# Paged value tiles of the merged stage requested by ScalarE instead of SyncE

## What is computed

```
qa, ka, va, ga, qb, kb, vb, gb, ma, mb = mixer_inputs(xs, ...)      # one projection of the input
for g, (win, dil) in enumerate(A_GROUPS):                           # (128,1), (512,4), (2048,16)
    k_ext = concatenate([buf[:, :, 0], ka[:, :, g]]); v_ext = concatenate([buf[:, :, 1], va[:, :, g]])
    o, lse = dilated_window_sample(qa[:, :, g], k_ext, v_ext, win, dil, slopes_a[g])
o_a = combine_groups(outs, lses)
pages = cache_b_kv[l][page_table]                                   # 16 pages a sequence
k_all = concatenate([past[:, :, 0], kb]); v_all = concatenate([past[:, :, 1], vb])
o_b = diff_attention(qb, k_all, v_all, ...)
y = x + (sigmoid(ma) * (silu(ga) * o_a) @ w_proj_a + sigmoid(mb) * (silu(gb) * norm(o_b)) @ w_proj_b) @ w_out
```

## Time and profile before

| | before |
|---|---|
| median of 3 runs | 1660.69 us (1660.46 to 1670.56) |
| profiled execution | 1662.41 us, its span 1660.4 us |
| PE busy | 96% of the span |
| ACT busy | 34% |
| DVE, POOL busy | 46%, 42% |
| DMA queue of SP (q1) | 308.55 MB, 61.6% of 16 engines' span |
| DMA queue of ACT (q10) | 58.92 MB, 10.7% |
| paged value tiles | 128 requests of 256 KB by SP |
| window value tiles | 96 requests by ACT, 8 by SP |

### The profile page before, as it was taken

One profiled execution on the slowest core, in us unless ns is written; L12 is line 12 of the kernel. 1 busy time (PEld: TensorE's weight loads), 2 busy tenths in 40 slices (PEclk: granted clock), 3 DMA queues, 4 the chain that ended last, 5 costly groups with the idle time before them and its releaser, 6 DMA issues.

```text
span 1660.4 us, 37307 instructions
## 1 busy us (share of the span) xinstructions
PE 1600.4 (96%) x14616; PEld 1371.5 (83%) x14616; DVE 756.4 (46%) x1852; ACT 564.6 (34%) x1341; POOL 699.3 (42%) x958
## 2 busy tenths in 40 slices
PE   6999999999999999999999999999899899999998
PEld 5787677878899999999999877778687788888787
DVE  5632576333473333733335554344354343588411
ACT  5321477121362213712136243343333244412300
POOL 5676340466533666446666112222121121666500
PEclk9999999999999999999999999999999999999999
DMA  5359897338983379933797899989888988865692
GB/s 164 111 148 188 274 310 222 102 87 153 269 274 91 83 165 257 307 105 104 173 276 241 281 311 319 301 282 319 286 292 295 324 261 254 293 197 171 196 329 95
DMA packets 351487, 369.84 MB, mean 223 GB/s; under 512 B 164113, under 2 KB 208274, under 8 KB 351314
## 3 DMA queue, kind: packets, MB, share of 16 engines
q1 hardware_dynamic: 306354, 308.55, 61.6%
q10 hardware_dynamic: 44960, 58.92, 10.7%
HBM read 310.83 MB, written 143.85 MB: 274 GB/s over the span
## 4 chain that ended last, share of the span: by engine, by line
PE 80%; DMA 4%; SPq 4%; DVE 4%; POOL 3%; issue 3%; ACT 2%; ACTq 0%; POOLq 0%; DVEq 0%
PE ps L2061 13%; PE ps L2063 13%; PE ps L2062 13%; PE ps L2114 4%; PE ps L2216 4%; PE ps L2115 4%; PE ps L2116 4%; PE ps L2273 4%; PE ps L2162 3%; PE ps L2236 3%; PE ps L2334 3%; PE ps L2223 2%; PE ps L2183 2%; DMA v_in<-in_cache_b_kv 2%; PE ps L2317 2%
## 5 line engine op out<-in xcount | busy, mean ns | idle before, releaser
L1058 POOL TENSOR_TENSOR w_lo<-raw,w_hi 128x512 fp32r<-128x512 f32 x140 | 181.7, 1302 | 410.7 <-ACT w_hi L1268 410.0
L2061 PE MATMUL ps<-w_hi,hT 128*128 128x512 f32 x824 | 333.0, 404 | 2.3 <-DVE w_lo L1574 1.3
L2063 PE MATMUL ps<-w_hi,hT 128*128 128x512 f32 x824 | 329.6, 400 | 0.0
L2062 PE MATMUL ps<-w_lo,hT 128*128 128x512 f32 x824 | 329.5, 400 | 0.0
L2114 PE MATMUL ps<-w_hi,hT 128*128 128x256 f32 x768 | 224.4, 292 | 4.4 <-issue 4.0
L2061 PEld LDWEIGHTS ps<-w_hi,hT 128*128 128x128 f32 x824 | 206.1, 250 | 23.5 <-DVE w_lo L1574 2.0
L2063 PEld LDWEIGHTS ps<-w_hi,hT 128*128 128x128 f32 x824 | 205.8, 250 | 20.4
L2062 PEld LDWEIGHTS ps<-w_lo,hT 128*128 128x128 f32 x824 | 206.5, 251 | 19.2
L2115 PE MATMUL ps<-w_lo,hT 128*128 128x256 f32 x768 | 216.9, 282 | 0.0
L2116 PE MATMUL ps<-w_hi,hT 128*128 128x256 f32 x768 | 216.2, 282 | 0.2 <-issue 0.2
L1112 POOL TENSOR_SCALAR qz<-qT,qcol 64x128 f32<-64x128 f32 x256 | 156.5, 611 | 108.1 <-PE ps L2162 54.5
(11 more groups left out here) (229 smaller groups left out, 2764.1 us busy)
## 6 DMA issues: line engine op xcount, KB each, us to landing
out<-in_cache_a_kv SPq DMA_DIRECT2D x32, 2040.0 KB, 13.6
k_in<-in_cache_b_kv SPq DMA_DIRECT2D x128, 256.0 KB, 4.0
v_in<-in_cache_b_kv SPq DMA_DIRECT2D x128, 256.0 KB, 6.1
raw<-in_w_in SPq DMA_DIRECT2D x104, 256.0 KB, 3.4
k_in<-in_cache_a_kv SPq DMA_DIRECT2D x104, 256.0 KB, 8.5
v_in<-in_cache_a_kv ACTq DMA_DIRECT2D x96, 256.0 KB, 6.5
out<-in_cache_a_kv SPq DMA_DIRECT2D x8, 2016.0 KB, 10.1
raw<-in_w_in ACTq DMA_DIRECT2D x40, 256.0 KB, 5.6
```

The costliest lines, as they stand in the source:

```text
L1058: pool.tensor_tensor(lo, raw_of(q), hi.bitcast(F32), ALU.subtract).then_inc(lo_done, 1)
L2061: pe.matmul(z, hi, wh, start=first, stop=False)
L2062: pe.matmul(z, hi, wl, start=False, stop=False)
L2063: return pe.matmul(z, lo, wh, start=False, stop=last)
```

## The change

`by_scalar(vv)` now says yes for every value tile but the first eight. ACT therefore requests the page tiles too, at the same place as it requests window tiles, and loads the page number for each itself. Ahead of its loop over the slots ACT waits for `first_in` to reach 48, that is, for the page table. SP loads page numbers for keys only, keeps nothing in `page`, and its wait for `s_pu` ahead of each value tile is gone, as no value tile beyond the first eight is left to it. The loads of the softmax statistics (`stc`), which stood in `load_values`, are a function of their own at the same place of SP's order.

```
         def by_scalar(vv):
 
-            return vv >= NVS and vv % TILES_S < TILES_A
+            return vv >= NVS
...
-            page = {}
-
             def rows_s(kk, kv):
                 b, T = divmod(kk, TILES_S)
                 if T >= TILES_A:
-                    if kv == 0:
-                        at_ = b * N_PAGES + T - TILES_A
-                        page[kk] = sp.value_load(pids[96:97, at_:at_ + 1], min_val=0, max_val=n_phys - 1)
-                    pid = page[kk] if kv == 0 else page.pop(kk)
+                    at_ = b * N_PAGES + T - TILES_A
+                    pid = sp.value_load(pids[96:97, at_:at_ + 1], min_val=0, max_val=n_phys - 1)
                     return cb[0, ds(pid, 1), :, kv].rearrange("o s h e -> (o s) (h e)")
...
             def load_values(vv):
-                if vv == TILES_S * (DEC_B - 1) + TILES_A + 7:
-                    sp.wait_ge(s_ta, DEC_B)
-                    sp.wait_ge(s_tb, DEC_B)
-                    for g in range(3):
-                        sp.dma_start(stc[:, :, g, :], st_scr[g].rearrange("(i p) s -> p i s", p=P)).then_inc(st_in, 16)
-                if vv >= NVS:
-                    sp.wait_ge(s_pu, piece_of(vv - NVS) + 1)
                 sp.dma_start(v_in(vv), rows_s(vv, 1)).then_inc(sv_in[vv % NVS], 16)
...
+            act.wait_ge(first_in, 48)
             for gg in range(SLOTS + 1):
...
                 for vv in values_freed(gg - 1):
                     if by_scalar(vv):
                         vb, T = divmod(vv, TILES_S)
-                        g, r = source_a(T)
+                        if T >= TILES_A:
+                            at_ = vb * N_PAGES + T - TILES_A
+                            pid = act.value_load(pids[96:97, at_:at_ + 1], min_val=0, max_val=n_phys - 1)
+                            rows = cb[0, ds(pid, 1), :, 1].rearrange("o s h e -> (o s) (h e)")
+                        else:
+                            g, r = source_a(T)
+                            rows = ca[g][0, vb, r::WINDOWS[g][1], 1].rearrange("m h e -> m (h e)")
                         act.wait_ge(s_pu, piece_of(vv - NVS) + 1)
-                        act.dma_start(v_in(vv), ca[g][0, vb, r::WINDOWS[g][1], 1].rearrange("m h e -> m (h e)"))\
-                            .then_inc(sv_in[vv % NVS], 16)
+                        act.dma_start(v_in(vv), rows).then_inc(sv_in[vv % NVS], 16)
```

More of the change, by code:

```diff
@@ L915, in load_keys, with load_stats @@
                 sp.dma_start(k_in[:, gg % NKS, j, :], rows_s(kk, 0)).then_inc(sk_in[gg % NKS][j], 16)
-            def load_values(vv):
-                if vv == TILES_S * (DEC_B - 1) + TILES_A + 7:
-                    sp.wait_ge(s_ta, DEC_B)
-                    sp.wait_ge(s_tb, DEC_B)
-                    for g in range(3):
-                        sp.dma_start(stc[:, :, g, :], st_scr[g].rearrange("(i p) s -> p i s", p=P)).then_inc(st_in, 16)
-                if vv >= NVS:
-                    sp.wait_ge(s_pu, piece_of(vv - NVS) + 1)
+            def load_stats():
+                sp.wait_ge(s_ta, DEC_B)
+                sp.wait_ge(s_tb, DEC_B)
+                for g in range(3):
+                    sp.dma_start(stc[:, :, g, :], st_scr[g].rearrange("(i p) s -> p i s", p=P)).then_inc(st_in, 16)
+            def load_values(vv):
                 sp.dma_start(v_in(vv), rows_s(vv, 1)).then_inc(sv_in[vv % NVS], 16)
@@ L940, in _ @@
                         load_values(vv)
+                    if vv == TILES_S * (DEC_B - 1) + TILES_A + 7:
+                        load_stats()
                 if gg % 8 == 4 and gg // 8 < DEC_B:
```

## The result

| | median of 12 runs | lowest to highest | profiled execution | its span | its mean granted clock |
|---|---|---|---|---|---|
| before | 1661.6 us | 1654.1 to 1670.6 | 1662.4 | 1660.4 | 0.991 |
| after | 1668.9 us | 1664.2 to 1677.7 | 1672.8 | 1670.7 | 0.985 |

The changed kernel takes 1.0042 times as long, with a 95% interval of 1.0024 to 1.0059. That is 7 us more, where 3.3 us less was predicted; the time lies inside the range. The profiled execution is 10.3 us longer than the one before, and 3.9 us above the median of its own kernel: its rows show mechanisms, and the sizes are taken from the runs further down.

A forecast was written before the change was run, and what follows sets the result against it. PE, 96% busy, could gain only from its idle time and its lowered clock. 7.9 us gained at p6 less 4.6 lost at the end makes 3.3: 1662.4 to 1659.1, less 1.7 for the median, 1657 us; range 1648 to 1670.

The forecast's parts named there:

- The price of a page tile: On ACT's queue: page number plus request take 1.17 us from one tile to the next, between 1.1 and 2.0 us.
- rival 1: On ACT, a page tile takes 1.4 us: gain 6, loss 11, so 1665 us; chance 0.15.
- rival 2: ACT's queue becomes the bound, at 2.0 us a tile: 35 us lost, 5 gained, 1690 us; chance 0.10.
- The gain at p6: Page tiles requested earlier: 4.3 us in four sequences, 2.1 in the tight one, 1.5 of clock; 7.9 us together.
- the other four sequences: Sequences with shorter page-tile waits at p6: 4.3 us together, 1.1 us each, all expected to go.
- The sequence of the rows: The tightest sequence, whose p6 wait the timeline shows whole: 3.67 us was to become some 1.6, 2.1 us gained.
- rival 4: Waits only change their name: page tiles land 2 us later, p6 waits stay, end costs 4.6; 1665 us, chance 0.13.
- may touch the third: Third cause of PE's waits in the merged stage, ACT's move of p3, 2.4 us: the change may affect it.
- The body at nothing: Later ACT moves and exponentials within the sequences cost nothing, covered by a gate unit of about 5.6 us.
- The start at nothing: ACT's page-table wait ahead of its loop holds the third gate unit's sigmoid 2 us at most, costing nothing.
- The end, 4.6 us: Late moves of p4 to p7 at the stage's end lose 0.7, 0.5, 0.7 and 2.7 us; between 2 and 7.
- The sum: 7.9 us gained at p6 less 4.6 lost at the end: 3.3 us gained.

The follow-up runs named there:

- e5: Changed kernel with T16 to T28 of the last sequence on SP, page numbers kept, and ACT's page-table wait at slot 7; 1657.9 us, ratio 0.9970 to before.
- e6: Kernel before, but ACT requests only T21 to T24 of the first seven sequences, with its page-table wait at slot 7; 1659.7 us, ratio 0.9975 to before.
- e2: Changed kernel with ACT's wait for the page table moved to slot 7, just ahead of its first page tile; 1666.1 us, ratio 1.0030 to before.
- e11: Kernel before with ACT moving p3 ahead of the split and the sigmoid of slot n=7; 1662.7 us, ratio 0.9989 to before.
- e8: Kernel before with only T16 to T28 of the last sequence requested by ACT, and the late page-table wait; 1672.2 us, ratio 1.0052 to before.
- e1: Changed kernel with T16 to T28 of the last sequence back on SP, which loads their page numbers again; 1665.4 us, ratio 1.0036 to before.
- e4: Changed kernel with each page number loaded twice on ACT, the second load unused; 1690.0 us, ratio 1.0190 to before.
- e9: Changed kernel with the late page-table wait and only T25 to T28 of the last sequence on SP, numbers kept; 1665.3 us, ratio 1.0011 to before.

## Why the prediction was right or wrong

- **The price of a page tile** was right: 283 ns for the number and 1.1 us from one tile to the next, against 1.17 forecast. Rivals 1 and 2 fell with it. (The Trainium skill's floor of about 600 ns for a tensor_load would make a tile 1.17 - 0.27 + 0.60 = 1.5 us, not the 1.4 of rival 1; the 283 ns measured decide against either.)
- **The gain at p6** was 7.9 us in the forecast; the runs give 5.0 (e5: 3.9 of work, 1.1 of clock). In the changed kernel's profile the other four sequences still wait 3.9 - 2.98 = 0.9 us, so 4.3 became 3.4. The sequence of the rows gained 0.7 instead of 2.1: T24 was requested as much earlier as forecast, but the four tiles landed after 5.7 us instead of 5.1 (median), T24 itself after 6.2, which is rival 4 in part. In e6 that sequence gained nothing. The waits for p3, of which the prediction only said "may touch the third", took 2.2 us back. Clock: 1.5 forecast, 1.1 found, within its error. The window tiles, 3.7 us better in this one profile, are no gain that I can show: e2 has the same body and waits 6.4 us for them, e5 4.5. Taken together the waits for value tiles are 12.6, 12.9 and 17.9 us in the three profiles with the old order of tiles in the body (before, e11, e8) and 4.8, 8.7, 8.3 and 7.0 in four with the new one (after, e1, e2, e5).
- **The body at nothing** ("All this I cost at nothing, covered by the gate unit") held in the main: no product waits for a late p4 or p5, and p7 (pT L1470 at L2316) costs 5.5 - 3.6 = 1.9 us in the two other sequences that wait there, for which the forecast had no term.
- **The start at nothing** ("holds the sigmoid of the third gate unit for 2 us at most, whose bank is wanted a unit later") failed. The sigmoid is 1.8 us late, as said, but its bank isn't all that waits for it: DVE takes the result before it turns `k_new`. The waits from 915 to 965 rise from 2.7 to 3.8 us. That wait is shown; its price isn't: e2 puts it at some 2 us, with an error that takes in nothing, and the fall of the clock there also comes without it.
- **The end, 4.6 us**, is the step that failed most: its work came out, and the clock that follows it was left out of the sum. e8 measures 4.6 us of work; that it is the very figure of the forecast is partly luck, as the terms differ. Of three small waits (p4, p5, p6: 1.9 us together) only 0.2 us at p6 came; one was larger: 3.6 us, for which I had 2.7, since p8's transposition wants p7's bank sooner than p7's own product. The clock then costs 4.0 us in e8 and 4.7 to 5.1 us in the changed kernel's trace. I had it only in the far end of the bound ("7 us, the clock falls once as well") and left it out of the sum, while I put 1.5 us of clock into the gain.
- **The sum**, with the sizes found: 5.0 - 8.6 - 2 = 5.6 us lost, against 7.3 measured between the medians. The forecast's 3.3 us gained fails by the clock at the end (4.0), the smaller gain (2.9) and the start (2, the least certain of the three).
- Of the rivals, none was it. Rivals 1 and 4 (both 1665) came nearest in time, by other ways: rival 1 by a dearer page number, rival 4 with the p6 waits unchanged.

What stays open: what the "issue" waits are (6.6 to 14.6 us, see above), and why window tiles are waited for 0.9 us in the changed kernel's profile and 6.4 us in e2's, which differs from it at the start alone. And how the cost of the nine tiles T16 to T24 at the end divides, which no run separated.

## What to carry to other kernels

Sum the two kinds of time apart: waits, and the clock that follows them. The change moved the work, which holds the waits, by only +0.5 us here, and the clock by 6.6. 4.0 us of that come with the end alone (e8), where one wait of 3.6 us stands in place of none. Before moving requests to an engine that computes, look for the place where its arithmetic is densest, follow who waits for each thing behind the requests (a bank that is still full, too, not only the next product), and leave that place alone; and see first whether the old queue can be put in a better order, which gave the same gain for nothing.

## What the runs showed of the hardware

- A page number took 283 ns on ACT's sequencer and 269 on SP's, a request with a register address 350 and 338: the two queues cost the same. But ACT's stand in order with its arithmetic, four tiles 4.3 us at a time (the move of p6 at 1169.6 starts 4.25 us after the one of p5 ended).
- Around a single idle time of 3.6 us PE's clock was at half for 10.2 us, though PE was busy from 1428.1 on; so in all three profiles with this wait. But the length of the wait doesn't give the price: waits of 5.3 and 4.3 us in e4 went with 6.8 us at half each, and waits of 0.64 and 1.91 us within 4 us (e9) with 6.8 us as well. At the end of the stage the stall's shadow cost more than the stall. The Trainium skill, page "TensorE: Matmul & The Clock Gate", section "Part 1: The HAM clock gate (the "warmup" mystery)", tells of the same two levels and that activity releases the lower one; the level of 0.50 here agrees.
- Runs of the kernel before differ by up to 16 us (1654 to 1671), their mean granted clock from 0.987 to 0.995; about half of the spread is the clock's. A profile of one run shows mechanisms, not a gain of 5 us.
